# A lead tensor that moves every SBUF tensor of a two-block layer kernel to new start addresses

## What is computed

```
# first block, per layer
z = rmsnorm(x) @ w_in + b_in                      # twelve parts of 1024 or 2048 columns
y_m = sigmoid(mo) * head_layernorm(mlstm_chunkwise(...))
y_r = silu(rg) * head_layernorm(retention_chunkwise(...))
x = x + (sigmoid(gm) * (y_m @ w_bm) + sigmoid(gr) * (y_r @ w_br)) @ w_out
x = x + square(relu(rmsnorm(x) @ w_ff1 + b_ff1)) @ w_ff2 + b_ff2
x = x + sigmoid(rmsnorm(x) @ w_pe_gate) * (p @ w_pe)
# second block, per layer: a mixer (gated linear attention and RWKV-7, or sparse attention), then
q = x @ w_q ; s = q . sub_keys ; idx, gate = top16 of 128 x 128 products of keys
h = gelu(x . expert_u[idx]) * gate ; x = layer_norm(ALPHA * x + h . expert_v[idx])
```

## Time and profile before

| | us |
|---|---|
| median of 3 runs | 3365.54 |
| lowest, highest | 3365.05, 3368.5 |
| profiled execution: span from first to last instruction | 3362.7 |
| TensorE busy in it | 3254.4 (97%) |
| LDWEIGHTS busy | 2853.6 (85%) |
| VectorE, ScalarE, GpSimd busy | 2153.4, 1499.6, 503.4 |

### The profile page before, as it was taken

One profiled execution on the slowest core, in us unless ns is written; L12 is line 12 of the kernel. 1 busy time (PEld: TensorE's weight loads), 2 busy tenths in 40 slices (PEclk: granted clock), 3 DMA queues, 4 the chain that ended last, 5 costly groups with the idle time before them and its releaser, 6 DMA issues.

```text
span 3362.7 us, 49470 instructions
## 1 busy us (share of the span) xinstructions
PE 3254.4 (97%) x20642; PEld 2853.6 (85%) x20642; DVE 2153.4 (64%) x3111; ACT 1499.6 (45%) x1717; POOL 503.4 (15%) x277
## 2 busy tenths in 40 slices
PE   8999999999999999989999999999999999999998
PEld 7787789797877896877999989888769999989886
DVE  6766665567666555685987754555677967655555
ACT  6444454464444544612444444444344344444443
POOL 0000000000000000010766600000003766200000
PEclk9999999989999999999999999999999999999999
DMA  5454644434545454403444465555424444555553
GB/s 221 147 185 163 214 165 181 164 139 162 186 163 211 167 184 157 160 18 113 173 163 151 148 247 190 184 188 188 171 88 151 176 154 148 209 213 181 187 188 124
DMA packets 87672, 565.19 MB, mean 168 GB/s; under 512 B 10176, under 2 KB 10192, under 8 KB 23584
## 3 DMA queue, kind: packets, MB, share of 16 engines
q1 hardware_dynamic: 80496, 534.81, 44.4%
q0 software_dynamic: 6960, 27.27, 2.4%
HBM read 552.60 MB, written 9.44 MB: 167 GB/s over the span
## 4 chain that ended last, share of the span: by engine, by line
PE 52%; DVE 5%; ACT 2%; issue 1%; POOL 1%; DVEq 0%; ACTq 0%
PE bank L1970 7%; PE bank L1971 7%; PE bank L1972 7%; PE bank L1991 7%; PE bank L1992 7%; PE bank L1993 7%; PE bank L1953 3%; ACT w_hi L2117 1%; PE bank L1678 1%; PE bank L1702 1%; PE bank L1679 1%; PE bank L1680 1%; PE bank L1704 1%; PE bank L1703 1%; POOL w_lo L1602 1%
## 5 line engine op out<-in xcount | busy, mean ns | idle before, releaser
L2117 ACT ACTIVATE w_hi<-raw 128x2048 fp32r<-128x2048 f32 x291 | 557.3, 1915 | 782.4 <-PE bank L1993 395.4
L2394 DVE TENSOR_TENSOR w_lo<-raw,w_hi 128x2048 fp32r<-128x2048 f32 x222 | 509.6, 2296 | 582.8 <-ACT w_hi L2117 582.0
L968 DVE TENSOR_TENSOR w_lo<-raw,w_hi 128x2048 fp32r<-128x2048 f32 x200 | 458.1, 2292 | 369.6 <-ACT w_hi L729 367.8
L729 ACT ACTIVATE w_hi<-raw 128x2048 fp32r<-128x2048 f32 x201 | 384.6, 1915 | 497.8 <-PE bank L483 340.7
L1970 PE MATMUL bank<-act_hi,w_hi 128*128 128x256 f32 x2048 | 590.2, 288 | 5.2 <-POOL w_lo L1602 5.2
L1971 PE MATMUL bank<-act_lo,w_hi 128*128 128x256 f32 x2048 | 578.6, 283 | 0.0
L1972 PE MATMUL bank<-act_hi,w_lo 128*128 128x256 f32 x2048 | 578.2, 282 | 0.0
L1991 PE MATMUL bank<-w_hi,c_hi 128*128 128x512 f32 x1024 | 405.0, 396 | 0.0
L1992 PE MATMUL bank<-w_lo,c_hi 128*128 128x512 f32 x1024 | 405.0, 395 | 0.0
L1993 PE MATMUL bank<-w_hi,c_lo 128*128 128x512 f32 x1024 | 405.0, 395 | 0.0
L1970 PEld LDWEIGHTS bank<-act_hi,w_hi 128*128 128x128 f32 x2048 | 391.3, 191 | 6.6 <-POOL w_lo L1602 6.4
(11 more groups left out here) (506 smaller groups left out, 5704.0 us busy)
## 6 DMA issues: line engine op xcount, KB each, us to landing
raw<-weights SPq DMA_DIRECT2D x492, 1024.0 KB, 4.8
row<-rows POOLq DMA_DIRECT2D x48, 256.0 KB, 4.2
spill<-staged SPq DMA_DIRECT2D x32, 256.0 KB, 2.9
hid<-spill SPq DMA_DIRECT2D x32, 256.0 KB, 4.9
y<-w_pe POOLq DMA_DIRECT2D x2, 1024.0 KB, 5.0
ln_row_mix<-ln_rows POOLq DMA_DIRECT2D x4, 512.0 KB, 4.9
hid<-keys POOLq DMA_DIRECT2D x2, 1024.0 KB, 6.4
ln_row_ffn<-ln_rows POOLq DMA_DIRECT2D x4, 512.0 KB, 7.7
```

The lines of the kernel that those rows point to most:

```text
L729: nc.scalar.activation(w_hi[:, k % SPLIT, :], raw[:, k % RAW, :], ACT.Copy).then_inc(hi_ready, 1)
L968: nc.vector.tensor_tensor(w_lo[:, k % SPLIT, :], raw[:, k % RAW, :], w_hi[:, k % SPLIT, :].bitcast(F32), ALU.subtract).then_inc(lo_ready, 1)
L2117: A.activation(hi_of(k), raw[:, k % RAW, :], ACT.Copy).then_inc(hi_ready, 1)
L2394: V.tensor_tensor(lo_of(k), raw[:, k % RAW, :], hi_of(k).bitcast(F32), ALU.subtract).then_inc(lo_ready, 1)
```

## The change

1. A tensor `lead` of 480 float32 (1920 bytes) is declared ahead of `raw`. It holds what `ident_sb` and `small` held, and the last part of the second block's constants (both rope tables of width 128 and three single columns). 16,512 + 1920 = 18,432 is a multiple of 2048.
2. A tensor `align_a` of 448 bytes, which nothing uses, is declared behind `eps_sb`.
3. The rope tables for width 64 go: `rope` reads every second column of the tables for width 128.
4. The constants of the second block come by three DMAs instead of two, and the waits on `b_const` are for 48 instead of 32.

```
-                  ("iota", P), ("causal", TT * S), ("cos128", TT * 64), ("sin128", TT * 64), ("cos64", TT * 32), ("sin64", TT * 32),
+                  ("iota", P), ("causal", TT * S), ("cos128", TT * 64), ("sin128", TT * 64),
...
+CONST_LEAD = CONST_B["cos128"][0]
+SMALL = 64
+LEAD = 480
...
         self.weights = weights
+        self.lead = sb("lead", [P, LEAD])
         self.raw = sb("raw", [P, RAW, TW])
...
-        self.ident_sb = sb("ident_sb", [P, P])
-        self.ident = self.ident_sb[:, :]
+        self.ident = self.lead[:, 0:P]
+        self.small = self.lead[:, P:P + SMALL]
+        self.const_lead = self.lead[:, P + SMALL:P + SMALL + CONSTS_B - CONST_LEAD]
...
     eps = eps_sb[:, :]
+    sb("align_a", [P, 112], F32, memory)
     attention = memory.enter_context(ExitStack())
...
-    const_rest = sb("const_rest", [P, CONSTS_B - CONST_EVEN])
+    const_rest = sb("const_rest", [P, CONST_LEAD - CONST_EVEN])
...
-        pool.dma_start(const_rest[:, :], consts_b[:, CONST_EVEN:CONSTS_B]).then_inc(b_const, 16)
+        pool.dma_start(const_rest[:, :], consts_b[:, CONST_EVEN:CONST_LEAD]).then_inc(b_const, 16)
+        pool.dma_start(const_lead, consts_b[:, CONST_LEAD:CONSTS_B]).then_inc(b_const, 16)
...
-        act.wait_ge(b_const, 32)
+        act.wait_ge(b_const, 48)
...
-            cos = bcast(cst(f"cos{width}")[:, t * w:(t + 1) * w].unsqueeze(1), [P, heads, w])
-            sin = bcast(cst(f"sin{width}")[:, t * w:(t + 1) * w].unsqueeze(1), [P, heads, w])
+            step = AD // width
+            cos = bcast(cst("cos128")[:, t * 64:(t + 1) * 64:step].unsqueeze(1), [P, heads, w])
+            sin = bcast(cst("sin128")[:, t * 64:(t + 1) * 64:step].unsqueeze(1), [P, heads, w])
```

More of the change, by code:

```diff
@@ L1328, in sem @@
         return ctx.enter_context(nc.semaphore(name))
-    const_rest = sb("const_rest", [P, CONSTS_B - CONST_EVEN])
+    const_rest = sb("const_rest", [P, CONST_LEAD - CONST_EVEN])
+    small, const_lead = m.small, m.const_lead
     def cst(name):
         first, n = CONST_B[name]
-        return const_even[:, first:first + n] if first < CONST_EVEN else const_rest[:, first - CONST_EVEN:first - CONST_EVEN + n]
-    small = sb("small", [P, 64])
+        if first < CONST_EVEN:
+            return const_even[:, first:first + n]
+        if first < CONST_LEAD:
+            return const_rest[:, first - CONST_EVEN:first - CONST_EVEN + n]
+        return const_lead[:, first - CONST_LEAD:first - CONST_LEAD + n]
     even = ExitStack()
@@ L2451, in _ @@
         do(V.memset(sh[:, :, 0:1], 0.0))
-        dve.wait_ge(b_const, 32)
+        dve.wait_ge(b_const, 48)
         dve.wait_ge(even_loaded, 48)
```

## The result

| us | before | changed |
|---|---|---|
| median (4 runs of each, on one chip) | 3365.3 | 3337.64 |
| lowest, highest | 3360.51, 3368.5 | 3334.71, 3343.18 |
| profiled execution, span | 3362.7 | 3332.9 |
| TensorE busy in it | 3254.4 | 3222.9 |

What follows compares the result with a forecast made beforehand. TensorE, busy 3254.4 of 3362.7 us, was taken as the bound. Terms -20.0 - 9.2 + 1.3 = -27.9 us took the 3365.5 us median to 3338 us; the 8-in-10 range was 3325 to 3360.

Steps and rivals of the forecast that it cites:

- The reason: 512-column matmuls: stationary slices starting on multiples of 128 bytes run 6.6 ns faster (226.7 against 233.3 ns).
- the offset to the moving operand in a finer pattern: Example cause within the rival that nothing moves: `mix` and `c` keep 233 ns, time stays 3365; chance 0.12.
- `c`, -20.0: Output stages: `c` put on a multiple of 128, 3072 matmuls at 6.6 ns less, taken as 20 us gained.
- `mix`, -9.2: 1536 matmuls with `mix` put on a multiple of 128, taken as 6 ns less each, 9.2 us gained.
- themselves wait for the end of a TensorE tile, so they move along: `mix` stages: VectorE and ScalarE steps that TensorE waits for would come earlier along with its tiles.
- The third slot, +1.3: Third weight slot moved to a multiple of 128: 672 matmuls of 256 columns lose 2 ns each, 1.3 us slower.
- Plain float32, 0: 1024 gate matmul records reading `hot_i` and `hot_j` stay at 274 ns, so 0 us.
- The large group, 0: 9312 matmuls of 256 columns, already on multiples of 128, move to multiples of 2048 at no cost: 0 us.
- The rival that put it out of step when both operands start alike: 9312 matmuls of 256 columns fall out of their steady 120 ns; slower, 3399 at 6.6 ns each; chance 0.05.
- One more issue on GpSimd, 0: An extra DMA issue of 0.53 us on GpSimd's queue delays `erow` under 5 us of slack: 0 us.
- Rope with a step of two, 0: Indexer's rope steps reading every second column stay at 414 ns: 0 us, at most 6.6 us if doubled.
- The signs that were named: Changed profile: 143 or 144 matmuls per window, means near 389 ns, 43.5 us stretches, 5.76 us third-slot tiles, 256-column means kept.

Runs made afterwards that it cites:

- e1: Kernel before plus two pads and shorter rope tables, no lead: `c`, `mix`, third slot on multiples of 128, `w` and `act` unmoved; 3359.11 us against 3362.7.
- e4: Changed kernel with all split operands 32 bytes further up, offsets between them kept; 3339.97 us, ratio 0.9925.
- e2: Changed kernel with `c` alone moved 32 bytes up; 3357.42 us, ratio 0.9981.
- e5: The kernel of e1 with longer pads, so all offsets are 0; no lead, no third constant DMA; 3335.91 us against 3363.6, ratio 0.9922.
- e6: Changed kernel with `act` 288 bytes up (weight minus activation 224) and a lead of 456; 3337.25 us, ratio 0.992.
- e7: Changed kernel with `c` 256 bytes up, `mix` 32 up, third slot 256 down; 3347.22 us in one run.
- e3: Changed kernel with `mix` alone (and what follows it in the first block) 64 bytes up; 3344.72 us, ratio 0.9938.
- e9: Changed kernel with `act` 64 bytes up, so weight minus activation is 192; 3326.21 us against 3360.31, ratio 0.9895.
- e12: Changed kernel with all weight slots, `mix` and `c` 192 bytes up, `act` not; 3333.25 us against 3362.67, ratio 0.991.
- e11: Changed kernel with `act` 192 bytes up, `mix` at 224, `c` at 160, third slot at 96 modulo 256; 3336.86 us in one run.
- e8: Changed kernel with `c` 192 bytes up, `mix` 448 up, third slot 320 down; 3353.08 us in one run.
- e10: Changed kernel with two places per weight slot, giving each matmul shape the offset that suits it; 3320.08 us against 3360.31, ratio 0.9876.

## Why the prediction was right, and its reason wrong

**What bounds.** Right. TensorE's stream set the end before and after; the idle time before lines 2002 to 2004 is still 0.0.

**The reason.** The step that failed is this one: "the stationary slices of `act` start on multiples of 128 bytes, those of `mix` at 64 past one, those of `c` at 32 past one", from which the text went on as if the multiple were the cause. e1 has all of them on multiples of 128 and stays at 232.4 ns; e4 has none there and runs at 227. What the three tensors differed in as well was the offset to the moving weight, at 128 past a multiple of 256: 0 for `act`, 64 for `mix`, 32 for `c`. The prediction named that ("the offset to the moving operand in a finer pattern"), but only as a way in which nothing would move. The change makes both true at once: its starts are multiples of 256, so the offsets are 0 (`side_hi`'s alone is not). The number came out right because of a property that the prediction didn't ask for. Had the change been e1, the same reasoning would have given 3338 and the runs 3359. The table of starts was enough to see that the two couldn't be told apart: the difference to the moving operand, 0, 64 and 32, has the same values as its column modulo 128, since `w` lay on a multiple of 128.

The Trainium skill, "Advanced Engine Details and Errata", section "Memory Cachelines", names lines of 16 bytes. By it alone all starts here are alike; the runs decide against it as the whole account, with 227 against 233 ns for starts that are all multiples of 32 (e2, e4).

**`c`, -20.0.** 18.9 us by the starts, 17.3 by the groups. Forecast was 6.6 ns from ten rows of a timeline; over all matmuls the difference is 233.2 - 227.0 = 6.2 ns, and 3072 x 6.2 = 19.0. A timeline rounds to 10 ns, so a mean of nine steps can be off by about 1 ns.

**`mix`, -9.2.** 7.6 us. The distance fell nearly as forecast, by 6.3 ns instead of 6.6. What is missing is a wait that takes a part back. `ffa2`'s stretch of 192 matmuls went from 44.67 us between first and last start to 43.77, 0.90 less instead of the 1.3 forecast. In the changed kernel a gap stands in it, where the third weight tile begins (timeline of TensorE; an ordinary distance is 0.23):

```profile
504.02 0.39 PE L489 MATMUL bank<-w_hi,mix_lo 128*128 128x512 f32 x1
504.53 0.50 PE L487 MATMUL bank<-w_hi,mix_hi 128*128 128x512 f32 x1
```

ScalarE's and VectorE's rows of the same stretch say who is late:

```profile
495.43 1.98 ACT L943 ACTIVATE conv<-bank,col 128x256 f32<-128x256 f32 x4
499.07 1.06 ACT L946 ACTIVATE mix_hi<-conv 128x1024 fp32r<-128x1024 f32 x1 [1.67 <-DVE conv L1283]
500.17 1.92 ACT L735 ACTIVATE w_hi<-raw 128x2048 fp32r<-128x2048 f32 x1
...
502.19 2.29 DVE L974 TENSOR_TENSOR w_lo<-raw,w_hi 128x2048 fp32r<-128x2048 f32 x1 [0.72 <-ACT w_hi L735]
```

ScalarE first finishes a later part of the stretch's stationary operand, splits the tile at 500.17, and VectorE ends `w_lo` at 502.19 + 2.29 = 504.48. That is 11.13 us after the stretch began at 493.35. Before it was 11.14 (505.60 + 2.29, from 496.75), but two tiles took TensorE 48 x 0.2333 = 11.2 us then and take 10.9 now. The prediction said that these steps "themselves wait for the end of a TensorE tile, so they move along". This one hangs on ScalarE's own work and does not move. It takes back 0.3 us here. The same gap of 0.51 us stands in all four stretches of 192, and in the two of 168 matmuls a wait grew from 1.13 to 1.43 us; over all 1536 matmuls the loss against 1536 x 6.3 = 9.7 us is 2.1 us.

**The third slot, +1.3.** +1.1. **Plain float32, 0.** 274 to 275 ns a record, 0.6 us in 1024. **The large group, 0.** 119.8 and 119.9 ns a distance. The rival that put it out of step when both operands start alike didn't come; its condition was no new one, since they had started alike before, at 128.

**One more issue on GpSimd, 0.** Right:

```profile
1325.22 0.53 POOL L1604 DMA_DIRECT2D erow<-erows  x1
...
erow<-erows POOLq DMA_DIRECT2D x1, 576.0 KB, 13.7
```

It lands at about 1338.9. ScalarE's step that needs it begins at 1344.76, 5.8 us later, where it was 5.

**Rope with a step of two, 0.** Right: 415 ns where it was 414.

```profile
L2843 DVE TENSOR_TENSOR qidx<-bank,lead 128x256 f32<-128x256 f32 x2 | 0.8, 415 | 0.0
```

This agrees with what the prediction cited from the Trainium skill, "SBUF — State Buffer", section "Door 1: The DMA port swizzle".

**The signs that were named.** Windows of 143 and 144: yes. Group means near 389: 390. Third-slot tiles at 5.76 us: 48 x 120.0. Groups 1970 and 523 unmoved: 289 and 287 ns. The stretches of `ffa2` and `ffb2` at 43.5 us: not quite, 43.7 to 43.8 from first to last start. The others came, and none of them could tell the reason given from the right one. Only a kernel in which multiple and offset part ways, as in e1 and e4, could.

**The number.** That the medians differ by 27.7 us where the sum said 27.9 is in part luck. The starts give 25.4, and the interval of the ratio is 4 us wide to either side. The 2.8 us that the text ahead put around the span were too much as well: a run's time is 1.8 us above its own span here (3334.71 against 3332.9), and the other 1.0 lay between two executions. The forecast went from median to median, so this doesn't touch it.

## What to carry to other kernels

For split matmuls of this form compare the starts of the two operands with each other, modulo 256 bytes, before looking at what either is a multiple of: two pads (e5) gave what the change gave. When a forecast rests on a property that the fast case has and the slow ones lack, list every property that does so, the relations between operands among them, and look for the kernel that separates them. When a stream gets faster, look for the first tiles behind a change of stage, where other engines are just in time on work of their own: there a part is given back (2 of 10 us against `mix`, next to none against `c`).

## What the runs showed of the hardware that was not expected

The distance between matmuls depends on the offset of the stationary to the moving operand, modulo 256 bytes. In ns, from the starts in the traces at clock 1.00:

| offset | 512 moving columns | 256 moving columns |
|---|---|---|
| 0 | 226.7 to 227.6 | 119.8 to 120.0 |
| 32 | 233.2 (before, e2, e6, e7) | 118.2 (before) |
| 64 | 233.3 (before, e3, e9, e12) | 113.3 to 117.8 by stretches, 115.3 in the mean (e11) |
| 128 | 232.3 to 232.5 (e1) | 118.6 (e1) |
| 160 | 233.3 (e11) | 120.0 (e11) |
| 192 | 228.8 to 229.3 (e8, e11) | 113.3 or 117.8 by stretches, 117.1 to 117.5 in the mean (e9, e10, e12); 113.3 (e8) |
| 224 | 233.3 (e11) | 116.9 (e6) |

The long shape wants the same remainder, by up to 2.8%; the short one is slowest there and at 160, and gains up to 3.9% in the mean of a kernel at other offsets, 5.6% where the 113.3 ns hold. A single rule that gives both columns wasn't found, and the offset alone doesn't fix the short shape: at 64 and 192 the same lines of one kernel run at 113.3 ns in some stretches and at 117.8 in others. What picks between them stays open. Whether data in bfloat16, or other shapes, show any of it wasn't tried.

A second thing: a faster stream can run into waits, and its clock fell with them. In e6 longer waits and a granted clock of 0.97 stand in the same 120 us of each expert layer, and take back some 14 of the 17 us that the distances gave; in e12 it is one layer, and in e9, as fast, neither.
